# Router logits of two token blocks in four column groups with a folding product, and the early gathers moved behind the third block's logits

## The reference

```python
mix = jnp.concatenate([y_conv, o.astype(x.dtype)], axis=-1) @ w_out
x = x + mix
x = x + moe(rmsnorm(x, norm_ffn_w), router_w, router_b, w_gate, b_gate, w_up, b_up, w_down, b_down)
...
logits = (t @ router_w + router_b).astype(jnp.float32)      # 32 experts
vals, idx = lax.top_k(logits, TOP_K)                        # top 4
gates = jax.nn.softmax(vals, axis=-1)
...
for e in range(N_EXPERTS):
    a = jnp.minimum((t @ w_gate[e] + b_gate[e]).astype(jnp.float32), SWIGLU_LIMIT)
    u = jnp.clip((t @ w_up[e] + b_up[e]).astype(jnp.float32), -SWIGLU_LIMIT, SWIGLU_LIMIT)
    hid = ((u + 1.0) * a * jax.nn.sigmoid(SWIGLU_ALPHA * a)).astype(t.dtype)
    y = y + combine[:, e:e + 1] * (hid @ w_down[e] + b_down[e]).astype(jnp.float32)
```

## Time and profile before

| | |
|---|---|
| Time, median of 3 runs | 1152.35 us (1152.32 to 1152.73) |
| The profiled execution | 1152.4 us, its span 1150.5 us |
| TensorE busy | 1108.7 us (96%) |
| VectorE, ScalarE, GpSimd busy | 400.1, 161.8, 23.7 us |
| Moved by DMA | 432.30 MB, mean 376 GB/s |
| Chain that ended last | TensorE 75%, DMA 21% |
| Granted clock of TensorE, mean | 0.997 |

### The profile page before, as it was taken

One profiled execution on the slowest core, in us unless ns is written; L12 is line 12 of the kernel. 1 busy time (PEld: TensorE's weight loads), 2 busy tenths in 40 slices (PEclk: granted clock), 3 DMA queues, 4 the chain that ended last, 5 costly groups with the idle time before them and its releaser, 6 DMA issues.

```text
span 1150.5 us, 15105 instructions
## 1 busy us (share of the span) xinstructions
PE 1108.7 (96%) x6045; PEld 464.8 (40%) x6045; DVE 400.1 (35%) x711; ACT 161.8 (14%) x283; POOL 23.7 (2%) x51
## 2 busy tenths in 40 slices
PE   8999999999999999999999999999999999999996
PEld 5786764433333333333333333333333333333332
DVE  4155185633333333333333332222233333333333
ACT  3100114311111111111111111111111111111112
POOL 0002000000000000000000000000000000000000
PEclk9999999999999999999999999999999999999998
DMA  9970308599999999999999999999999999999992
GB/s 314 332 219 1 147 28 331 228 405 430 414 426 434 434 432 431 432 432 431 433 433 428 433 434 427 434 433 428 433 434 428 433 434 430 431 435 432 430 426 101
DMA packets 35389, 432.30 MB, mean 376 GB/s; under 512 B 2527, under 2 KB 17699, under 8 KB 21797
## 3 DMA queue, kind: packets, MB, share of 16 engines
q1 hardware_dynamic: 33712, 428.13, 89.0%
q0 software_dynamic: 848, 3.03, 0.7%
q10 hardware_dynamic: 805, 0.82, 0.2%
HBM read 428.26 MB, written 3.71 MB: 375 GB/s over the span
## 4 chain that ended last, share of the span: by engine, by line
PE 75%; DMA 21%; ACT 2%; DVE 2%; issue 0%; SPq 0%; ACTq 0%; DVEq 0%
PE ps L1339 44%; DMA ring<-in_w_gate 21%; PE ps L1073 9%; PE ps L1316 5%; PE ps L1190 3%; PE ps L1238 3%; PE ps L1325 2%; PE ps L1382 2%; PE ps L1241 2%; ACT R L577 1%; PE ps L1063 1%; PE ps L1100 1%; PE ps L1298 1%; DMA consts<-in_consts 0%; PE ps L1208 0%
## 5 line engine op out<-in xcount | busy, mean ns | idle before, releaser
L1339 PE MATMUL ps<-ring,R 128*64 128x512 f32 x3072 | 690.0, 595 | 13.2 <-DMA ring<-in_w_gate 13.2
L1339 PEld LDWEIGHTS ps<-ring,R 128*64 128x64 f32 x3072 | 209.8, 136 | 410.8 <-issue 382.1
L930 DVE SCALAR_TENSOR_TENSOR x<-ps,gates,x 128x1024 f32<-128x1024 f32 (+1 forms) x96 | 106.2, 1106 | 133.7 <-PE ps L1316 133.7
L1073 PE MATMUL ps<-R,ring 128*128 128x320 f32 x384 | 107.4, 436 | 0.6 <-DVE R L657 0.6
L936 DVE TENSOR_TENSOR R<-ps,R 128x512 f32<-128x512 f32 x32 | 22.1, 692 | 240.4 <-ACT R L580 240.4
L969 DVE TENSOR_SCALAR R<-ps 128x512 f32<-128x512 f32 x32 | 22.1, 692 | 187.9 <-PE ps L1339 187.9
L1073 PEld LDWEIGHTS ps<-R,ring 128*128 128x128 f32 x384 | 71.7, 190 | 31.1 <-issue 1.8
L1316 PE MATMUL ps<-R 64*128 64x512 bf16 (+1 forms) x576 | 79.3, 381 | 0.0
L573 ACT ACTIVATE R<-R 128x512 f32<-128x512 f32 x32 | 20.2, 632 | 307.4 <-DVE R L967 307.4
L1316 PEld LDWEIGHTS ps<-R 64*128 64x128 bf16 (+1 forms) x576 | 21.4, 98 | 88.8 <-issue 51.9
L557 ACT ACTIVATE R<-ps 128x512 f32<-128x512 f32 x33 | 19.7, 598 | 234.3 <-PE ps L1241 234.3
(11 more groups left out here) (220 smaller groups left out, 601.3 us busy)
## 6 DMA issues: line engine op xcount, KB each, us to landing
ring<-in_w_gate SPq DMA_DIRECT2D x30, 4096.0 KB, 28.4
ring<-in_w_up SPq DMA_DIRECT2D x28, 4096.0 KB, 29.3
ring<-in_w_down SPq DMA_DIRECT2D x28, 4096.0 KB, 31.1
ring<-in_w_up SPq DMA_DIRECT2D x8, 2048.0 KB, 11.7
ring<-in_w_down SPq DMA_DIRECT2D x8, 2048.0 KB, 12.7
ring<-in_w_in SPq DMA_DIRECT2D x14, 1024.0 KB, 12.6
ring<-in_w_gate SPq DMA_DIRECT2D x4, 2048.0 KB, 9.7
ring<-in_w_out SPq DMA_DIRECT2D x4, 1024.0 KB, 8.9
```

Of the source, the lines that this page charges most:

```text
L930: STT(xb[b], rows, gates[:, par, b:b + 1], xb[b], ALU.mult, ALU.add).then_inc(accDone, 1)
L1073: ins = MM(ps[:, n % 2, 0:NT], slot_k(L, 256)[:, k, 128 * half:128 * half + 128], hT[:, k, :], start=(k == 0), stop=(k == KT - 1))
L1339: ins = MM(shape(ps[64 * half:64 * half + 64, bank, :]), lhs(k), cols(w, half), start=False, stop=(k == KT - 1))
```

## The change

The logits of blocks 0 and 1 are formed the other way round: `rw` (128x32) is stationary in one of four column groups (k-tile k in group k % 4) and `x2T` (128 columns) moves. That gives four partial sums, transposed, on 4 x 32 partitions (`logit_parts`). ScalarE copies them to SBUF (`keep_parts`), and one product with `fours`, four unit matrices of 32 below each other, adds the four and turns them back (`sum_logits`). Block 2 keeps `logits`. The turned copy of block 1 moves to ScalarE. The third part of block 1 moves from VectorE to GpSimd and counts a new semaphore, `h2Rest`. `add_mixer(2)` moves ahead of `place(0)` on VectorE. On TensorE the order behind `wout(1)` is new.

```diff
+        lgPart = view(R3, 2048, shape=(128,))
+        fours = sb("fours", [128, E])
...
+            pool.wait_ge(partDone, 4)
+            pool.wait_ge(resid, 2)
+            pool.tensor_tensor(h2p[:, 2, 1, :], h2f[:, 1, :], h2p[:, 1, 1, :], ALU.subtract).then_inc(h2Rest, 1)
             pool.wait_ge(woutMM, 3)
...
+            def keep_turned():
+                act.wait_ge(x2TMM, 2)
+                act.wait_ge(lgPartMM, 1)
+                act.activation(x2T.rearrange("p k t -> p (k t)"), ps[:, 6:8, :].rearrange("p a n -> p (a n)"), ACT.Copy)\
+                    .then_inc(x2TOut, 1)
+            def keep_parts(b):
+                act.wait_ge(lgPartMM, b + 1)
+                if b:
+                    act.wait_ge(lgMM, b)
+                act.activation(lgPart, ps[:, 1, 0:128], ACT.Copy).then_inc(lgPartOut, 1)
...
             part(0, 1)
+            keep_parts(0)
             square2(1)
             root2(1)
+            keep_turned()
             part(1, 0)
+            keep_parts(1)
             part(1, 1)
...
-            did(TT(fold[:], ident[:, 0:64], ident[:, 64:128], ALU.add), foldOut)
+            need(did(TT(fold[:], ident[:, 0:64], ident[:, 64:128], ALU.add), foldOut))
+            did(TT(fours[:], fold[:, 0:32], fold[:, 32:64], ALU.add), foldOut)
...
             choose(0)
-            keep_turned(1)
             norm_rows(1)
             remainder(1, 0)
             choose(1)
-            remainder(1, 1)
+            add_mixer(2)
             place(0)
             place(1).then_inc(earlyP, 1)
-            add_mixer(2)
             keep_turned(2)
...
+            def logit_parts(b):
+                pe.wait_ge(x2TOut, b + 1)
+                pe.wait_ge(rwOut, 1)
+                if b:
+                    pe.wait_ge(lgPartOut, b)
+                for k in range(KT):
+                    j = k % 4
+                    ins = MM(ps[32 * j:32 * j + 32, 1, 0:128], rw[:, k, :], x2T[:, k, :], start=(k < 4), stop=(k >= 4))
+                ins.then_inc(lgPartMM, 1)
+            def sum_logits(b):
+                pe.wait_ge(lgPartOut, b + 1)
+                pe.wait_ge(foldOut, 2)
+                MM(ps[:, LGB[b], E * b:E * b + E], lgPart, fours[:], start=True, stop=True).then_inc(lgMM, 1)
...
             def gather_block(b):
-                pe.wait_ge(h2Parts, b + 1)
+                pe.wait_ge(h2Parts, min(b + 1, 2))
...
-            logits(0)
+            logit_parts(0)
+            wout(2, range(2))
+            sum_logits(0)
             turn_x2(1)
-            wout(2, range(KT // 2))
-            logits(1)
-            wout(2, range(KT // 2, KT - 2))
+            wout(2, range(2, 4))
+            logit_parts(1)
+            wout(2, range(4, 6))
+            sum_logits(1)
+            wout(2, range(6, KT))
+            tails()
             positions(0)
             positions(1)
-            wout(2, range(KT - 2, KT))
-            pe.wait_ge(earlyP, 1)
-            gather_block(0)
             turn_x2(2)
...
+            stay_busy(2)
+            logits(2)
+            pe.wait_ge(earlyP, 1)
+            gather_block(0)
+            pe.wait_ge(h2Rest, 1)
             gather_block(1)
-            logits(2)
-            tails()
-            stay_busy(7)
+            stay_busy(2)
             positions(2)
```

More of the change, by code:

```diff
@@ L216, in hybrid_shortconv_hgrn2_moe_step @@
         rwOut = sem("rw_out")
+        h2Rest = sem("h2_rest")
+        lgPartMM, lgPartOut = sem("lg_part_mm"), sem("lg_part_out")
         vSelDone, s0Scaled, tailIn, biasDone, biasPart, biasRest, ehDone = (sem("vsel_done"), sem("s0_scaled"), sem("tail_in"),
@@ L800, in keep_turned @@
                 dve.wait_ge(x2TMM, b + 1)
-                if b:
-                    dve.wait_ge(lgMM, b)
-                if b < 2:
+                if b == 0:
                     dve.tensor_copy(x2T, ps[:, 6:8, :].rearrange("p a (k t) -> p (a k) t", t=128)).then_inc(x2TOut, 1)
                 else:
+                    dve.wait_ge(lgPartMM, 2)
                     dve.tensor_copy(x2T[:, :, 0:64].rearrange("p (h c) t -> p h c t", h=2),
```

## The result

The changed kernel takes 1155.09 us (median of 19 runs, 1152.65 to 1158.01), the kernel before beside it 1152.54 (19 runs, 1151.25 to 1154.78): a ratio of 1.0022, 95% interval 1.0014 to 1.0029, so 2.5 us slower. The forecast was 1.5 us. The profiled execution took 1154.9 us, with a span of 1153.1 (1152.4 and 1150.5 before).

A forecast was written before the change was run, and what follows sets the result against it. The first expert's start, from which the DMA weight stream never pauses, was taken to set the end. The second gather's wait (1.4 us) and the start (0.1) on 1152.35 gave 1153.8 us, range 1151.4 to 1156.0.

The forecast's parts named there:

- What bounds it: Expert loop: the weight stream's anchor is the DMA issue at 247.24, so the first expert's start (222.39) sets the end.
- The logits: Blocks 0 and 1 on TensorE: 3.9 us removed, 2.4 added, so wout(2) ends at 210.1 instead of 211.56.
- Rival D: New logits: the four column groups run in series, giving 1155.8 us; it or another larger stall: chance 0.08.
- GpSimd's hold: GpSimd's subtraction holds choose(1)'s VectorE instruction until 210.5; keep_turned(2) begins at 212.6, only 0.44 us early.
- The forecast's other end: choose(1) on VectorE not held by GpSimd: keep_turned(2) at 211.9, positions(2) 0.7 us later, 1153.1 us.
- The h2Parts wait: Second gather waits for remainder(2, 1), block 2's last piece: positions(2) starts at 218.65 instead of 217.28, 1.4 us later.
- The clock: TensorE's clock was taken not to fall in its 2.2 us stop ahead of the second gather; a fall was a rival.
- rival C: TensorE's stop ahead of the second gather halves the clock up to the first expert: 4 us more, 1158; chance 0.12.
- Here it is dense: Argument against a clock fall at the second gather: TensorE's work before the stop is dense, unlike at the kernel's end.
- The extra operation for fours: Start of the kernel, on VectorE behind fold: near 0.2 us, of which some 0.1 is carried through.
- The sum of 1.5 us: Whole kernel: 1.4 us at positions(2) plus 0.1 at the start, on the median 1152.35, gives 1153.8 us.
- the chance given to that side: Slower by more than 0.2%: 0.21, made of rival C, Rival D and a twentieth for an added half microsecond.

The follow-up runs named there:

- e4: The kernel before with 25 instead of 5 filler products between block 2's slot numbers and the wait ahead of the first expert: 1156.78 us, ratio 1.0035.
- e5: The kernel before, with SyncE's load issued at 211.70 also waiting for the slot numbers of block 2: 1152.65 us, ratio 0.9995.
- e3: The changed kernel, block 1's gather waiting for its own parts only and GpSimd's subtraction starting after choose(1): 1151.92 us, ratio 0.9989.
- e2: The changed kernel with ten filler products ahead of the waiting second gather: 1153.93 us, ratio 1.0013.
- e7: The changed kernel with fillers ahead of block 2's turning (5), its logits (4 instead of 2) and the second gather (10): 1153.73 us, ratio 1.0013.
- e10: The kernel before with eight more filler products in TensorE's idle places of the first 14 us: 1152.02 us, ratio 0.9997.
- e12: The changed kernel with eight early fillers (first 14 us), plus fillers ahead of block 2's turning, its logits and the second gather: 1153.55 us, ratio 1.0008.
- e11: The changed kernel with eight more filler products in the first 14 us and nothing else: 1154.73 us, ratio 1.0021.
- e6: The kernel before with only the new logits of blocks 0 and 1; remainder on VectorE, gathers and add_mixer(2) where they were: 1152.84 us, ratio 1.0001.
- e8: The changed kernel, block 1's gather waiting for its own parts, its remainder in VectorE's gap, choose(2) ahead of block 2's remainders: 1151.28 us, ratio 0.9984.

## Why the prediction was right, and where it was short

- **What bounds it** held. `e4` moved the start by 4.3 us and the end by about 4; `e5` moved the load by 6.4 us (net of the constant) and the end not at all.
- **The logits** held: 0.57 and 0.58 us up to the next row (0.68 forecast), the folding products 0.25 and 0.34 (0.53 forecast), wout(2) at 209.92 (210.1). Rival D, column groups one after another, is out. Its working has a slip: two times 1.2 us less the 1.5 gained is 0.9, not 1.1; it touches the upper bound alone.
- **GpSimd's hold** held: 2.12 us (1.98), the held operation until 210.72 (210.5), keep_turned(2) at 212.48 (212.6). The forecast's other end, after the Trainium skill (SBUF — State Buffer, Who interferes with whom), was that GpSimd is the one to wait if VectorE's instruction starts first. No run here shows that: in `e3` a semaphore held GpSimd back, and the place's tensor_scalar was held instead. The same section of the Trainium skill names tensor_scalar among those that can take the shared port; the trace of `e3` agrees (1.20 against 0.33 us).
- **The h2Parts wait** held in place and kind: idle 2.31 us (2.2), second gather at 217.39 (217.43 by the forecast's own steps), cost 1.0 to 1.2 us against the kernel before (1.4).
- **The clock** is the step that failed, though the number came out within the range. It was rival C at 0.12, and it came in the profiled execution, and by the mean clocks in most others: 11 of the 19 runs were at 0.994 or less, where none of the 97 of the kernel before was, and with the start filled all 11 were below the lowest of the kernel before with its start filled. Two arguments were wrong. "Here it is dense": TensorE was busy for only 0.92 of the 2.00 us from 210 to 212 (2.00 before), idle places that the forecast didn't have, and `e2`, with the stall filled, fell 2.1 us behind them. And the one such stop known, at the end of the kernel, was set aside as different. Its price was mis-sized the other way, "4 us more": from the second gather to the first expert it is 8.93 us, against 6.32 in `e7`, so 2.6; 2.0 at the first expert itself, as `e7`'s fillers overrun; 1.2 to 1.8 in the median. The clock was back at 223.5, 2.8 us ahead of the first expert, and not all of that stretch is work of TensorE.
- **The extra operation for fours**: the first projection begins at 13.45 instead of 13.28, near the forecast 0.1; but it begins at 13.82 in `e10`, which doesn't have it. So no run shows the term.
- The sum of 1.5 us was somewhat high for what it held (the version without the fall, `e12`, is 1.5 above `e10`, or 1.0 without the fillers' overrun), and the clock put 1.2 to 1.8 on top. The median 1155.09 lies in the range, 1.3 us above the forecast. That is in part luck: the range left C out on purpose, C came, and by its own price of 1158 the time would have been outside. The whole, 0.22%, stands just beyond the 0.2% that was called no change; the chance given to that side, 0.21, should be 0.24 by its own terms (0.12, 0.08 and a twentieth of 0.80).

## What to carry to other kernels

A shared counter that was harmless as a wait on an engine's past becomes a wait on its future when one of its increments moves to another engine: look at each waiter of that counter, by what is last to reach the number. Where TensorE has to wait, the price can be the wait and the clock behind it; count the idle places just ahead as well, and fill them, but not past the end of the wait. Before a difference of 1 us is read from two profiled executions, take out the constant that is already there where the change begins.

## What the runs showed of the hardware

- A half clock lasted 6.8 us behind the 2.31 us stop (changed kernel), and about 3.4 us in `e11` and `e2` and near the start of `e4`, `e5`, `e6` and `e8`. It fell 1.5 us after the last product in one (215.08 to 216.6), and in the other two with TensorE at work again: at 218.8 in `e11`, 1.2 us after the second gather had begun, and at 214.0 in `e2`. The same program falls in some executions and not in others, by the mean clocks: 0.997 or more in 52 runs of the kernel before, 0.995 or 0.996 in 45. With only the idle place of 0.72 or 0.70 us ahead of positions(1) left, the traces of `e7` and `e12` show no fall from 205 to 228, and the mean clocks of their 22 runs are 0.996 to 0.998.
- VectorE beside a GpSimd tensor_tensor: a tensor_tensor of two SBUF inputs took 1.82 instead of 0.29 us; a tensor_scalar with one SBUF input, float32 to bf16, 1.20 instead of 0.33; a tensor_tensor with one PSUM input 0.69, not held; a FIND_INDEX8 (0.18 us at 208.68 in the changed kernel, as before) not held either. The held tensor_scalar was not expected.
